# First projection of a two-network transformer kernel: shared key tiles, value slabs by halves of the rows, and two changed seams

## The reference

```
first network, per layer:
  u = rmsnorm(h)
  aq, ak, av, iq, ik, iw, bq, bk, bv, cq, ck, cv, gates = split(u @ w_in)
  ik = rope(rmsnorm(ik)); all q and k = rope(...)
  o_a = attention over the 128 best keys, picked by sum_h iw_h * relu(iq_h . ik)
        (6 heads, one shared key head ak and value head av; 8 indexer heads, one shared key ik)
  o_b = dilated attention (12 heads);  o_c = window of 128 with sinks (8 heads, 2 key heads ck)
  h += (g0 * (o_a @ w_a) + g1 * (o_b @ w_b) + g2 * (o_c @ w_c)) @ w_o
  h += relu(rmsnorm(h) @ w_up)^2 @ w_down
second network, per layer:
  mix = [stick-breaking, latent-key softmax, RWKV-7](x @ w_in);  x = layernorm(alpha x + mix @ w_o)
  x = layernorm(alpha x + (gelu(conv(x @ up)) * (x @ gate)) @ w_down)
```

## Time and profile before

| | |
|---|---|
| median of three runs | 3486.25 us |
| the profiled execution | 3484.35 us |
| its span, first to last instruction | 3482.6 us |
| mean granted TensorE clock | 0.979 |
| first projection, layer 0 | 30.97 to 247.3 us |
| first projection, layer 1 | 950.11 to 1165.6 us |

### The profile page before, as it was taken

How to read it: one execution, slowest core, us unless ns; L and a number is a source line. 1 busy time by engine, 2 the same in 40 slices (tenths; PEclk the granted TensorE clock), 3 DMA queues, 4 the chain that set the end, 5 groups by cost and what they waited for, 6 DMA issues and landing times. The chain is left out here.

```text
span 3482.6 us, 55438 instructions
## 1 busy us (share of the span) xinstructions
PE 3354.8 (96%) x22920; PEld 2758.1 (79%) x22920; DVE 1715.5 (49%) x2672; ACT 1351.9 (39%) x2057; POOL 958.1 (28%) x631
## 2 busy tenths in 40 slices
PE   8999999999999899999999999899999999899998
PEld 6777887888777778878887759888887758898887
DVE  4887434404249763341312656454444566454454
ACT  4646333313255452332224353343324453343322
POOL 2325002434433330034443341141101332141100
PEclk9999999999999999999999999999999999899999
DMA  3210222222222012222223200112222200112222
GB/s 142 85 37 27 90 103 87 97 97 97 97 97 73 1 65 92 101 86 103 90 104 121 73 1 4 76 60 96 97 97 92 96 2 3 47 65 97 96 97 73
DMA packets 42852, 267.04 MB, mean 77 GB/s; under 512 B 6912, under 2 KB 9344, under 8 KB 11904
## 3 DMA queue, kind: packets, MB, share of 16 engines
q1 hardware_dynamic: 42624, 263.74, 21.4%
HBM read 261.63 MB, written 2.10 MB: 76 GB/s over the span
## 5 line engine op out<-in xcount | busy, mean ns | idle before, releaser
L1446 POOL TENSOR_TENSOR w_lo_f<-raw_f,w_hi_f 128x2048 fp32r<-128x2048 f32 x60 | 275.7, 4596 | 383.9 <-ACT w_hi_f L390 383.9
L402 PE MATMUL ps<-u_hi,w_hi_d 128*128 128x512 f32 (+1 forms) x768 | 290.6, 378 | 7.9 <-POOL u_lo L2882 6.2
L403 PE MATMUL ps<-u_lo,w_hi_d 128*128 128x512 f32 (+1 forms) x768 | 286.8, 373 | 0.0
L404 PE MATMUL ps<-u_hi,w_lo_d 128*128 128x512 f32 (+1 forms) x768 | 286.7, 373 | 0.0
L390 ACT ACTIVATE w_hi_f<-raw_f 128x2048 fp32r<-128x2048 f32 x64 | 121.9, 1908 | 254.9 <-PE ps L404 243.8
L402 PE MATMUL ps<-u_hi,w_hi_f 128*128 128x512 f32 x512 | 201.4, 393 | 6.6 <-POOL u_lo L340 6.6
L620 POOL TENSOR_TENSOR w_lo_a<-raw_a,w_hi_a 128x2048 fp32r<-128x2048 f32 x30 | 137.9, 4598 | 229.9 <-ACT w_hi_a L616 229.9
L403 PE MATMUL ps<-u_lo,w_hi_f 128*128 128x512 f32 x512 | 201.0, 393 | 0.0
L404 PE MATMUL ps<-u_hi,w_lo_f 128*128 128x512 f32 x512 | 200.6, 392 | 0.0
L402 PE MATMUL ps<-hid_hi,w_hi_f 128*128 128x512 f32 x512 | 199.2, 389 | 0.0
L403 PE MATMUL ps<-hid_lo,w_hi_f 128*128 128x512 f32 x512 | 199.2, 389 | 0.0
(11 more groups left out here) (443 smaller groups left out, 8578.7 us busy)
## 6 DMA issues: line engine op xcount, KB each, us to landing
raw_d<-in_w SPq DMA_DIRECT2D x70, 1024.0 KB, 4.8
raw_f<-in_w SPq DMA_DIRECT2D x64, 1024.0 KB, 4.8
raw_c<-in_w SPq DMA_DIRECT2D x40, 1088.0 KB, 5.0
raw_a<-in_w SPq DMA_DIRECT2D x36, 1024.0 KB, 4.8
raw_p<-in_w SPq DMA_DIRECT2D x22, 1024.0 KB, 4.9
wo_raw<-in_w SPq DMA_DIRECT2D x4, 1024.0 KB, 5.9
h<-in_x SPq DMA_DIRECT2D x8, 256.0 KB, 4.6
mla_w<-in_w SPq DMA_DIRECT2D x2, 1024.0 KB, 6.9
```

Source lines behind the costliest of these rows:

```text
L402: nc.tensor.matmul(out, w_hi, x_hi, start=start, stop=False)
L403: nc.tensor.matmul(out, w_hi, x_lo, start=False, stop=False)
L404: return nc.tensor.matmul(out, w_lo, x_hi, start=False, stop=stop)
L1446: nc.gpsimd.tensor_tensor(WF[2][:, k % 2, :], WF[0][:, k % 2, :], WF[1][:, k % 2, :].bitcast(F32), ALU.subtract).then_inc(S["w_lo"], 1)
```

## The change

- The four tiles with keys held twice become two: `SHARED_TILE = {0: 4, 25: 26}`. Tile 0 has `ik` in its lower and `ak` in its upper half, tile 25 the two `ck` heads; tiles 4 and 26 are not made by TensorE. The slabs are put together by the transfers, from pieces of the weights in memory (`w1_pieces`). The rope of such a tile ends in four adds in place of one, which write both halves of both tiles.
- The indexer's products begin at place 4 of the tile list for 5.
- A value pair is fetched as rows 0 to 511 of both slabs and then rows 512 to 1023; `values` goes over its four banks twice, and needs only the first slab for the first time. The first value block moves 456 columns for 512. The slab behind the first value slab is split after `v_half`.
- `ik_sum` and the norm of the key come after the first four chunks of the first value tile.
- `arriving` gives, at the six starts, first the two matmuls per tile that need `u_hi` alone, then `wait_low`, then the third.
- The counts of banks of two blocks are made by SP.
- The first half of the output projection's slab 0 (second network) is split inside the steps `LAST` of the block before: ScalarE behind ("hi", 2), VectorE ahead of ("var", 4).

```diff
-        SLABS = (0, S1_V, S1_V + 3, 2, 3, 4, 13, 1, 5, 6, 7, 8, 9, 10, 11, 12, S1_V + 1, S1_V + 2)
+        SLABS = (0, S1_V, S1_V + 3, 2, 3, 4, 12, 1, 5, 6, 7, 8, 9, 10, 11, S1_V + 1, S1_V + 2)
+        SHARED_TILE = {T_IK: T_AK, T_CK: T_CK + 1}
+        V_WIDTH = (2 * 256 - 56, 2 * 256)
...
+        def arriving(pe, tiles):
+            for c in range(DC):
+                pe.wait_ge(S["u_hi"], c + 1)
+                for out, w_hi, w_lo in tiles:
+                    nc.tensor.matmul(out, w_hi[:, c, :], u_hi[:, c, :], start=(c == 0), stop=False)
+                    nc.tensor.matmul(out, w_lo[:, c, :], u_hi[:, c, :], start=False, stop=False)
+                wait_low(pe, c)
+                ms = [nc.tensor.matmul(out, w_hi[:, c, :], u_lo[:, c, :], start=False, stop=(c == DC - 1)) for out, w_hi, w_lo in tiles]
+            return ms
...
+        def w1_pieces(layer, i):
+            k = SLABS[i]
+            to = WA_raw[:, i % 4, :].rearrange("p (k c) -> p k c", c=256)
+            of = lambda k: d["w1"][layer:layer + 1, k, :, 0:2048].rearrange("a p (k c) -> p (a k) c", c=256)
+            if k >= S1_V:
+                first = i if i % 2 else i - 1
+                to = WA_raw[:, i % 4, :].rearrange("p (k c) -> p k c", c=512)
+                rows = slice((i - first) * DC // 2, (i - first + 1) * DC // 2)
+                return [(to[:, :, 256 * e:256 * (e + 1)], of(SLABS[first + e])[:, rows, :]) for e in range(2)]
+            shared = [(t, o) for t, o in SHARED_TILE.items() if t // 2 == k]
+            if not shared:
+                return [(to, of(k))]
+            t, o = shared[0]
+            a, b = t % 2 * P + HD, o % 2 * P
+            at = [(slice(0, a), k, slice(0, a)), (slice(a, a + HD), o // 2, slice(b, b + HD)), (slice(a + HD, 256), k, slice(a + HD, 256))]
+            return [(to[:, :, x], of(j)[:, :, y]) for x, j, y in at if x.start < x.stop]
...
-            TILES = [t for k in SLABS if k < S1_V for t in (2 * k, 2 * k + 1) if t < N_QK]
+            of_slab = lambda k: [t for t in (2 * k, 2 * k + 1) if k < S1_V and t < N_QK and t not in SHARED_TILE.values()]
+            TILES = [t for k in SLABS for t in of_slab(k)]
-            INDEX_AT = [5 + i for i in range(len(INDEX))]
+            INDEX_AT = [4 + i for i in range(len(INDEX))]
...
                 if i < len(SLABS):
-                    act.wait_ge(landed[i % 4], 16 * (i // 4 + 1))
-                    if i >= 3:
+                    act.wait_ge(landed[i % 4], landings(i))
+                    if i - 3 == VPAIR[0]:
+                        act.wait_ge(S["v_half"], 1)
+                    elif i >= 3:
...
+                        for kh in range(2):
+                            slab_ready(pe, i + kh)
...
+                            for tb in range(TB):
+                                b = bank_to_fill(pe, jobs, ("v", s, tb)) if kh == 0 else jobs.at["v", s, tb][0]
+                                tok = slice(tb, L, TB) if s == 1 else slice(tb * P, (tb + 1) * P)
+                                for k in range(DC // 2):
+                                    c = kh * DC // 2 + k
+                                    m = product3(ps[:, b, 0:V_WIDTH[s]], u_hi[:, c, tok], u_lo[:, c, tok], w_hi[:, k, :], w_lo[:, k, :],
+                                                 c == 0, c == DC - 1)
+                                if kh == 1:
                                     m.then_inc(full[b], 1)
+                                elif (s, tb) == (0, TB - 1):
+                                    m.then_inc(S["v_half"], 1)
+                                if (s, kh, tb) == (0, 0, 0):
+                                    b = bank_to_fill(pe, jobs, "ik_sum")
+                                    pe.wait_ge(S["ik_squared"], 1)
+                                    nc.tensor.matmul(ps[:, b, :], blk, iksq, start=True, stop=True).then_inc(full[b], 1)
...
                             s = VPAIR.index(i)
+                            if s == 0:
+                                norm_root(act, jobs, "ik_sum", rstd)
+                                act.wait_ge(S["ik_normed"], 1)
+                                swap(1, ikn)
+                            split_a_hi(act, jobs, i + 3)
                             for tb in range(TB):
...
-                        nc.vector.tensor_tensor(qk[:, t, :], qk[:, t, :], halves[:, i % 2, :], ALU.add)\
-                          .then_inc(S["roped"], 1)
+                        if t in SHARED_TILE:
+                            lower, upper = slice(0, HD), slice(HD, P)
+                            for to, row, frm in ((SHARED_TILE[t], upper, upper), (SHARED_TILE[t], lower, upper), (t, upper, lower)):
+                                dve.wait_ge(*own.up(nc.vector.tensor_tensor(qk[row, to, :], qk[frm, t, :], halves[frm, i % 2, :],
+                                                                            ALU.add)))
+                            nc.vector.tensor_tensor(qk[lower, t, :], qk[lower, t, :], halves[lower, i % 2, :], ALU.add)\
+                              .then_inc(S["roped"], 1)
...
                         if step == ("hi", 2):
+                            act.wait_ge(S["ahead"], 32)
+                            nc.scalar.activation(WO_hi[:, 0, 0:FIRST], W2[0][:, 0, 0:FIRST], ACT.Copy).then_inc(S["part_hi"], 1)
...
+                        if step == ("var", 4):
+                            dve.wait_ge(S["part_hi"], 1)
+                            nc.vector.tensor_tensor(WO_lo[:, 0, 0:FIRST], W2[0][:, 0, 0:FIRST], WO_hi[:, 0, 0:FIRST].bitcast(F32),
+                                                    ALU.subtract)
...
+                    banks_counted(sy)
...
-                    for b in range(8):
-                        pe.sem_inc(full[b], 1)
-                        pe.sem_inc(read[b], 1)
```

More of the change, by code:

```diff
@@ L428, in build @@
         squares8 = place("squares8", 13256, DC, L)
-        def w1_slab(layer, k):
-            return d["w1"][layer:layer + 1, k].rearrange("a p c -> p (a c)")
+        def w1_pieces(layer, i):
[14 more added lines that the diff above has]
+            return [(to[:, :, x], of(j)[:, :, y]) for x, j, y in at if x.start < x.stop]
+        AHEAD_DMAS = 1 + sum(len(w1_pieces(0, i)) for i in range(AHEAD))
         def fetch_next(sy, layer):
@@ L580, in last_of, with landings @@
                 k = SLABS[i]
-                return ("t", min(2 * k + 1, N_QK - 1)) if k < S1_V else ("v", int(i > VPAIR[0] + 1), TB - 1)
+                return ("t", of_slab(k)[-1]) if k < S1_V else ("v", int(i > VPAIR[0] + 1), TB - 1)
+            def landings(i):
+                return 16 * sum(1 if j < AHEAD else len(w1_pieces(0, j)) for j in range(i % 4, i + 1, 4))
             jobs = Banks(count=6)
@@ L2700, in _ @@
                 def _(pe, jobs=jobs):
-                    for b in range(8):
-                        pe.sem_inc(full[b], 1)
-                        pe.sem_inc(read[b], 1)
                     def wo(half, n):
-                        if half == 0 and n == 0:
-                            pe.wait_ge(S["part_lo"], 1)
-                        elif half == 0 and n % 2 == 0:
+                        if half == 0 and n in (2, 4, 6):
                             pe.wait_ge(S["w_lo"], n // 2 + 1)
```

144 lines of the change are left out of this document (63 added, 81 removed).

## The result

The changed kernel took 3435.30 us as the median of four runs (3435.16 to 3437.23), the kernel before 3485.36 us beside it (3483.46 to 3487.79): ratio 0.9857, 95% interval 0.9845 to 0.9869. The forecast was 3435. The profiled execution took 3435.26 us with a span of 3433.5, 49.1 us less than the span before; 51.0 were forecast.

The account below looks back on a forecast made before the run. TensorE, busy for 96% of the span, was taken as the bound. First projections 42, up-projection starts 2.8, second network's starts 3.8 and output seams 2.4 sum to 51.0 us saved: 3435 as a median, own range 3430 to 3441.

Parts of the forecast that it names:

- TensorE's sum: First projection: removed tiles, narrower columns, shorter waits and fewer slow matmuls save TensorE 22.0 us per layer.
- VectorE "level with TensorE": First projection: VectorE ends at 224.5 to 226.5, level with TensorE; 1 us taken off, leaving 21 us per layer.
- signs of being right: Included the block after the first projection coming 21 us earlier, VectorE ending within 2 us of TensorE.
- The walk through the queues: First projection: VectorE's score operations meet GpSimd's splits six times for eight, waiting 8 to 9 us less.
- The adds on an operand in PSUM: Shared tiles' extra adds, reading PSUM, don't wait for GpSimd; otherwise 4.5 us per layer lost, sum 33 for 42.
- The starts: Six projection starts: reordering saves 1.3 to 1.4 us at four, 1.9 us at the second network's two.
- The output projection's seam: Second network: the first half slab split a block earlier, TensorE waiting for SP's counts, saves 1.2 us, twice 2.4.
- Transfers in pieces: First projection's slabs fetched in pieces: cost 0 to 1.4 us once at the kernel's start, taken as 0.
- clock eats half: Part of rival 2: the low clock takes back half of what the earlier starts gain.
- Rival 1: First projection: VectorE becomes last as most meetings with GpSimd recur; 37 us saved, 3449; chance 0.20.
- rival 2: ScalarE's splits stay queued behind swaps, a 3 to 4 us wait stays at the second value pair; 3452; chance 0.12.
- rival 3: Slab 12 in pieces lands so late that TensorE and ScalarE stand still in early tiles; slower, 3490; chance 0.03.

Follow-up runs that it names:

- The kernel in which VectorE is out of the way: Changed kernel with the relu kept in PSUM, index products handled ahead of the next tile's swaps and rope, 3 search steps per tile: 3431.13 us, ratio 0.9843.
- Starts: Changed kernel, but at the six starts TensorE waits for `u_lo` ahead of each chunk's first matmuls again: 3445.49 us, ratio 0.9881.

## Why the prediction was right

**TensorE's sum, 22.0 us per layer: right.** Add what TensorE waits more at the block's end (3.48 - 0.94 = 2.5) to what the stretches and the start show: 17.9 + 1.35 + 2.5 = 21.8 us in layer 0, 17.1 + 1.35 + 2.5 = 20.9 in layer 1. The kernel in which VectorE is out of the way gives 22.5 and 21.2. The terms: tiles 10.9 for 10.9; columns 1.8 for 2.4 (the width counts, but not in full); the starts' waits 1.35 for 1.3; the pair's wait 4.3 and 4.0 for 4.3, and with its clock 7.3 and 5.6 for 6.6.

**VectorE "level with TensorE", 1 us off: the mis-sized term.** It is 2.5 us per layer. The first projections gave 37.7 us (17.9 + 17.1 + 2 x 1.35) where 42 were forecast; VectorE's end is 3.0 of the difference, TensorE's sum 1.3, about what the columns fell short by. Two of the forecast's signs of being right were missed with it: VectorE was to end within 2 us of TensorE and ended 3.3 us behind the start of its last matmul, 2.9 behind that one's end; and the next block came 19.3 and 18.4 us earlier for 21. The walk through the queues had the meetings right. Six groups of score operations are long, as forecast; over their undisturbed durations of 1.07, 1.33 and 1.60 us they wait 14.8 us, where the kernel before waited 23.6: 8.8 us less for "8 to 9". (The forecast put that waiting at 12 to 18 us. It counted the 21 operations of one line; 7.2 of the 23.6 us are in three other ones, with a single tensor operand.) What it lacked is the 107.23 row above. VectorE had caught up with its supply and stood idle for 2.4 us, waiting for ScalarE's swaps of a tile that TensorE had only just made; before there was no idle stretch of 0.3 us behind 106.66. From the first long meeting to its last operation VectorE took 129.9 us for 136.0. That is 6.1 us less and not 8.5 (8.8 less the 0.3 of the extra adds). The difference is this idle stretch, of the same length in layer 1; that is read from the trace, no run tested it by itself. Nor was the place of `ik_sum`, or the index products' place alone, undone by itself. The forecast also let the next block begin the moment VectorE ends; it begins 0.56 us later.

**The adds on an operand in PSUM: right.** They take 0.69 us each in the changed kernel, beside GpSimd's work too. Its split runs from 109.69 to 114.28; the last add runs within it and is not held up, and the next operation, with both operands in SBUF, is (3.23 us for 0.48):

```profile
109.69 4.59 POOL L656 TENSOR_TENSOR w_lo_a<-raw_a,w_hi_a 128x2048 fp32r<-128x2048 f32 x1 [8.03 <-ACT w_hi_a L652]
```

```profile
110.72 0.68 DVE L820 TENSOR_TENSOR qk<-qk,ps 64x512 f32<-64x512 f32 x1
111.33 3.23 DVE L844 SCALAR_TENSOR_TENSOR score<-four,iw,score 128x256 f32<-128x256 f32 x1
```

**The starts: right.** 1.35 us for 1.3 to 1.4 at four places (12.9 to 7.5 us of wait), 2.1 for 1.9 at two (8.0 to 3.8). Undoing them all costs 8.1 to 8.4 us in the medians.

**The output projection's seam: a little better than forecast.** 4.4 us of wait became 2.73, so 1.7 us each for 1.2. SP counts behind its two fetches, as forecast, and the wait for it is the rest; the low part of the moved half slab costs the block before nothing.

**Transfers in pieces at nothing: right**, by the kernel with whole slabs.

**The clock.** The forecast took 2.3 us for the slow matmuls behind the second value pair in each layer and left the rest as a rival's "clock eats half". The clock's sum over the two first projections fell by 5.4 us for the 4.6 of the forecast. It did not eat half of the starts: the slow stretches behind them are no longer than before (see "Starts").

So the sum of 51.0 met 49.1 in spans: 4.3 us too much for the first projections, 1.0 too little at the output projection's two seams, 0.3 at the starts, and 0.6 us by which the very first matmuls of this execution began earlier (26.07 for 26.70). The rest, 0.5 us, is not resolved.

Part of this is luck. Row by row the table of distances does not close so well: up-projection and down should show two later starts, 3.4 us, and shows 0.9; the second network's layer 1 should show one seam, 1.7 us, and shows 4.9, with 5.5 us less in the clock's sum of one block. These swings of the clock happen to cancel. And the median of 3435 was met to 0.3 us because the forecast put it 1.9 us above the profiled execution, as in the kernel before; it came 0.04 above it, which made good the 1.9 us by which the sum was too large.

Rival 1 (VectorE last) was the right mechanism at about a fifth of its price (3.0 of 14 us); rival 2 fell with the two `w_lo_a` rows; rival 3 with the whole slabs.

## What to carry over

When two engines end a block within a few microseconds of each other, a wait that one loses is not its gain: walk the queue forward and look for the idle stretch that appears where it has caught up with its supply. An operand moved out of a shared port's reach frees the operation but can tie up something else, here a bank until the slower engine has read it; order the reader's queue so that it frees before it does its long work. And judge an edit of a few microseconds by the stretch that it touches, before the median, and let that stretch begin behind the matmuls that the low clock slows: here that took its scatter from 1.5 us to 0.1.

## What the runs showed of the hardware

- The mutual exclusion with GpSimd moves rather than vanishes: once the 24 score operations were free, three adds of 128x128 on two SBUF operands rose from 0.29 to 3.19 us each.
- Reading the relu from PSUM costs nothing in the operation with two tensor operands (0.48 us for 256 columns, as undisturbed from SBUF), but the one with a single tensor operand, which starts each row, went from 0.35, 0.41 and 0.48 us to 0.48, 0.61 and 0.75.
- An operation with one tensor operand can wait for GpSimd as well when that operand is in SBUF: 3.92 us for 0.41 beside a split from 126.56 to 131.16.
- An add over 64 partitions takes as long as one over 128: 687 ns for both.
- TensorE's low clock behind the same gaps differs between executions of nearly the same code. The clock's sum ran from 59 to 71 us in these kernels, several us of it in blocks that the edits don't touch. The same 48 matmuls of a start took from 12.38 to 13.89 us.
